# One doubling level fewer, running sums in halves, and a gate column block moved in a two-layer hybrid mixer

## The reference, cut to what matters

```python
p = rms_norm(x, norm_g) @ w_in                  # columns: sb, mla, rwkv, merge gates
# A) stick-breaking attention: between = reverse cumulative sum of log_fail over the keys
w = where(causal, exp(log_beta + between), 0);  y_sb = w @ v
# B) latent attention, softmax over chunk-causal scores
# C) RWKV-7: state = state * w_t + (state @ a_t) b_t + v_t k_t;  o_t = state @ r_t
merged = g_sb * (y_sb @ w_br_sb) + g_mla * (y_mla @ w_br_mla) + g_rw * (y_rw @ w_br_rw)
x = x + merged @ w_out
```

## Time and profile before

| | us |
|---|---|
| median of three runs | 1707.79 (1707.07 to 1709.06) |
| the profiled execution | 1707.07 |
| its span in the trace | 1705.3 |
| PE busy | 1690.0 |
| DVE busy | 1123.4 |
| ACT busy | 839.6 |
| POOL busy | 494.2 |

### The profile page before, as it was taken

One profiled execution on the slowest core, in us unless ns is written; L12 is line 12 of the kernel. 1 busy time (PEld: TensorE's weight loads), 2 busy tenths in 40 slices (PEclk: granted clock), 3 DMA queues, 4 the chain that ended last, 5 costly groups with the idle time before them and its releaser, 6 DMA issues.

```text
span 1705.3 us, 22326 instructions
## 1 busy us (share of the span) xinstructions
PE 1690.0 (99%) x8522; PEld 1409.5 (83%) x8522; DVE 1123.4 (66%) x1531; ACT 839.6 (49%) x1197; POOL 494.2 (29%) x728
## 2 busy tenths in 40 slices
PE   8999999999999999999999999999999999999999
PEld 7878888888878888888888788888888888888887
DVE  4667565755977556786656775756569666578853
ACT  6544454434544454555454444534445454555532
POOL 1011212410352426362410112232205334244500
PEclk9999999999999999999999999999999999999999
DMA  8866656556656556795687555556465555668764
GB/s 249 266 181 182 181 160 185 163 166 177 177 175 183 163 180 219 229 310 195 204 264 226 175 182 170 178 161 186 148 180 174 177 164 172 195 209 276 272 195 157
DMA packets 176914, 332.82 MB, mean 195 GB/s; under 512 B 19516, under 2 KB 32746, under 8 KB 176808
## 3 DMA queue, kind: packets, MB, share of 16 engines
q1 hardware_dynamic: 165416, 297.07, 57.2%
q0 software_dynamic: 9584, 33.47, 5.9%
q10 hardware_dynamic: 1808, 0.86, 0.2%
HBM read 311.18 MB, written 16.78 MB: 192 GB/s over the span
## 4 chain that ended last, share of the span: by engine, by line
PE 93%; DVE 4%; ACT 1%; DMA 1%; issue 1%; SPq 0%; ACTq 0%; DVEq 0%
PE D L698 83%; PE B L698 9%; DVE w_lo L1394 1%; DMA ring<-in_w_in 1%; DVE arena L1394 1%; ACT arena L1018 0%; ACT w_hi L1018 0%; DVE xy L1394 0%; PE B L890 0%; PE B L771 0%; DVE arena L1599 0%; DVE gev L1440 0%; PE B L869 0%; ACT gev L1018 0%; ACT L1018 0%
## 5 line engine op out<-in xcount | busy, mean ns | idle before, releaser
L1394 DVE TENSOR_TENSOR w_lo<-ring,w_hi 128x1024 fp32r<-128x1024 f32 (+3 forms) x560 | 677.6, 1221 | 357.5 <-ACT w_hi L1018 349.9
L1018 ACT ACTIVATE w_hi<-ring 128x1024 fp32r<-128x1024 f32 (+3 forms) x560 | 574.7, 1038 | 445.5 <-PE D L698 342.1
L698 PE MATMUL D<-w_hi,ht_hi 128*128 128x512 f32 (+2 forms) x1728 | 683.9, 396 | 4.1 <-DVE w_lo L1394 4.1
L698 PE MATMUL D<-w_hi,ht_lo 128*128 128x512 f32 (+2 forms) x1728 | 667.4, 386 | 0.0
L698 PE MATMUL D<-w_lo,ht_hi 128*128 128x512 f32 (+2 forms) x1728 | 666.6, 386 | 0.0
L698 PEld LDWEIGHTS D<-w_hi,ht_hi 128*128 128x128 f32 x1728 | 326.3, 189 | 71.8 <-issue 9.6
L698 PEld LDWEIGHTS D<-w_hi,ht_lo 128*128 128x128 f32 x1728 | 325.6, 188 | 65.7
L698 PEld LDWEIGHTS D<-w_lo,ht_hi 128*128 128x128 f32 x1728 | 326.4, 189 | 58.7 <-issue 0.5
L600 POOL COPY arena<-arena 32x256 f32<-32x256 f32 x240 | 168.7, 703 | 141.6 <-DVE arena L1424 105.9
L698 PEld LDWEIGHTS B<-arena 128*66 128x66 f32 (+3 forms) x1440 | 144.1, 163 | 25.5 <-issue 6.9
L1018 ACT ACTIVATE arena<-B 64x128 f32<-64x128 f32 (+5 forms) x162 | 54.5, 342 | 220.5 <-PE B L698 215.1
(11 more groups left out here) (156 smaller groups left out, 1380.5 us busy)
## 6 DMA issues: line engine op xcount, KB each, us to landing
ring<-in_w_in SPq DMA_DIRECT2D x368, 512.0 KB, 4.4
ring<-in_w_out SPq DMA_DIRECT2D x64, 512.0 KB, 5.4
ring<-in_w_br_mla SPq DMA_DIRECT2D x32, 512.0 KB, 5.1
gate_spill<-gev POOLq DMA_DIRECT2D x24, 512.0 KB, 4.7
arena<-gate_spill POOLq DMA_DIRECT2D x24, 512.0 KB, 5.8
ring<-in_mla_w_ukv SPq DMA_DIRECT2D x16, 512.0 KB, 4.2
ring<-in_w_br_rw SPq DMA_DIRECT2D x16, 512.0 KB, 5.2
ring<-in_w_br_sb SPq DMA_DIRECT2D x16, 512.0 KB, 5.0
```

The costliest lines, as they stand in the source:

```text
L698: return nc.tensor.matmul(o, a, b, start=start, stop=stop, skip_group_check=True)
L1018: return nc.scalar.activation(o, i, fn, **kw)
L1394: return v.tensor_tensor(o, a, b, op)
```

## The change

- The levels start from the inverse of 4x4 blocks instead of 2x2: `LEVELS` is 5, and DVE makes that inverse (products with three shifted diagonals, a reduction, transposes, six short operations, then a product of 512 columns and two sums). PE's first level visit stands 5 chunks behind the scores.
- The operands of both running sums are written as two fp32r halves (by DVE), the constants `inc`, `ntri`, `none` become an fp32r tile that POOL fills; twice as many matmuls in one pass each. The factor of the decay moves into ACT's scales.
- mg0 stands between sv and gate10: mg0 now ends at 184, gate10 at 192, gate11 at 200.
- The stick-breaking visits stand at 190, 194, 196.5 and 199, 202.5, 205.5. POOL does move(0) after mla pair 1; after move_heads(0) it goes to the end of gate10 (waits for its take-out and issues its spill), does all of move(1), and then enters the first pair with move_heads(1). `turn_heads` writes to a tile of its own.
- At the start SP's queue carries x and the first weights in turn (x0, w0, x1, w1, x2, w2, x3), and ACT and DVE split the first chunk ahead of the first columns.

```diff
-LEVELS = 6
-LEVELS_IN = 5
+LEVELS = 5
+LEVELS_IN = 4
...
-    g += wide("sq", C_SB) + pair(2) + wide("sk", C_SB + 512) + pair(3) + wide("sv", C_SB + 1024) + gates[10:]
-    g += wide("mg0", C_MG) + wide("mg1", C_MG + 512) + wide("sg", C_SB + 1536)
+    g += wide("sq", C_SB) + pair(2) + wide("sk", C_SB + 512) + pair(3) + wide("sv", C_SB + 1024) + wide("mg0", C_MG)
+    g += gates[10:] + wide("mg1", C_MG + 512) + wide("sg", C_SB + 1536)
...
-RW_STEPS = [1, 1.3, 1.2] + [0.9, 1] * LEVELS + [1] * 6
+RW_STEPS = [1, 1.2, 1, 1.5, 1.8] + [0.88, 0.98] * LEVELS + [0.85] * 6
...
-ML_STEPS += ML_PREP + ML_VISITS + [0.8] * 6 + ML_VISITS
-SB_STEPS = [4, 3.5, 3]
+ML_STEPS += ML_PREP + ML_VISITS + [1.05] * 6 + ML_VISITS
+SB_STEPS = [2.9, 1.2, 2.9, 2.7]
...
 sync:
             for j in range(4):
                 first_x(j)
+                if j < LEAD:
+                    first_chunk(j)
...
 gpsimd, layer 0:
+                    pool.dma_start(SUMS_IN, consts[:, K_END:K_END + 3 * P]).then_inc(sums_loaded, 16)
...
+                    nc.gpsimd.tensor_copy(sums_of[:], SUMS_IN.rearrange("p (n c) -> p n c", n=3)).then_inc(sums_in, 1)
...
 gpsimd, attention:
-                    if p == 0:
+                    if p == 1:
                         move(0)
                     beat(9)
...
                 move_heads(0)
-                dense_to(END["sv"])
+                dense_to(END["gate10"])
+                move(1)
                 for q in range(SBH // 2):
 
                     if q == 0:
                         move_heads(1)
-                    else:
-                        move(1, range(2))
-                    beat(2)
+                    beat(3)
                     for e in range(2):
                         pool.wait_ge(sb_act, 8 * l + 4 * q + 3 + e)
...
                     beat()
-                    if q == 1:
-                        pool.wait_ge(sb_pool, 4 * l + 4)
-                        move(1, range(2, 4))
...
 tensor, rw_pair:
-                beat()
-                beat()
+                beat(4)
                 for n in range(1, LEVELS + 1):
...
 tensor, sb_pair:
-                beat()
+                beat(2)
                 for e in range(2):
-                    lf, o = LF[e], B[2 * e + 1]
+                    o = B[2 * e + 1]
                     pe.wait_ge(sb_dve, 8 * l + 4 * q + e + 1)
-                    mm(o[:, 0:256], ntri, lf[:, 0:256], False, True)
-                    mm(o[:, 128:256], none, lf[:, 256:384], False, True)
-                    mm(o[:, 256:384], ntri, lf[:, 256:384], False, True).then_inc(sb_pe, 1)
+                    for lf in (LFH[e], LFL[e]):
+                        mm(o[:, 0:256], ntri, lf[:, 0:256], False, False)
+                        mm(o[:, 128:256], none, lf[:, 256:384], False, False)
+                        last = mm(o[:, 256:384], ntri, lf[:, 256:384], False, True)
+                    last.then_inc(sb_pe, 1)
...
 tensor, decay sums:
+                pe.wait_ge(sums_in, 1)
+                pe.wait_ge(sig_split, 2 * l + 2)
                 for h in range(HALVES):
-                    mm(B[h][:], con[:, K_INC:K_INC + P], SIG[:, h, :], True, True)
+                    mm(B[h][:], inc, SIGH[:, h, :], True, False)
+                    mm(B[h][:], inc, SIGL[:, h, :], False, True)
...
 scalar, start:
-            for n in range(LEAD):
-                for d0, m, src in pieces(0, n, 0):
-                    act.dma_start(ring[:, n, :, d0:d0 + m], src).then_inc(first_w[n], 16)
...
-                    columns_hi(0, first_pe, first_xh)
                     first_split(0)
+                    columns_hi(0, first_pe, first_xh)
...
 vector, rw_pair:
-                link(tt(WC, UC, first_c.unsqueeze(1).to_broadcast([P, 4, 32]), ALU.mult))
+                link(tt(WIDE[:, 0:3], UC.unsqueeze(1).to_broadcast([P, 3, 4, 32]), over_units(3), ALU.mult))
+                link(v.tensor_reduce(DIAG[:, :, 0:4], WIDE[:, 0:3], axis=X, op=ALU.add))
+                link(v.transpose(DIAG_T, DIAG))
+                d1, d2, d3 = (DIAG_T[:, k, :] for k in range(3))
+                t1, t2 = WIDE[:, 3, 0, :], WIDE[:, 3, 1, :]
+                tt(t1[:, 0:31], d1[:, 0:31], d1[:, 1:32], ALU.mult)
+                link(tt(t2[:, 0:30], d2[:, 0:30], d1[:, 2:32], ALU.mult))
+                tt(d2[:, 0:31], d2[:, 0:31], t1[:, 0:31], ALU.add)
+                link(tt(d3[:, 0:30], d3[:, 0:30], t2[:, 0:30], ALU.add))
+                link(tt(t1[:, 0:31], d1[:, 0:31], d2[:, 1:32], ALU.mult))
+                link(tt(d3[:, 0:31], d3[:, 0:31], t1[:, 0:31], ALU.add))
+                link(v.transpose(INVERSE[:, 0:3, :], DIAG_T))
+                beat()
+                link(tt(WIDE, over_columns(INVERSE, 4), over_units(4), ALU.mult))
+                link(tt(WIDE[:, 0:2], WIDE[:, 0:2], WIDE[:, 2:4], ALU.add))
+                link(tt(WC, WIDE[:, 0], WIDE[:, 1], ALU.add))
...
 vector, sb_pair, in the loop over e:
-                    last.then_inc(sb_dve, 1)
-                beat(2)
+                    link(last)
+                    link(v.tensor_copy(LFH[e], LF[e]))
+                    tt(LFL[e], LF[e], LFH[e].bitcast(F32), ALU.subtract).then_inc(sb_dve, 1)
+                    beat()
+                beat()
```

More of the change, by code:

```diff
@@ L63 @@
 LEAD = HALF_RING - 1
-ARENA = 19900
+ARENA = 20690
 SB_SCALE = 128.0 ** -0.5
@@ L76 @@
 K_END = K_COL + 2
+K_INC, K_NTRI, K_NONE = K_END, K_END + P, K_END + 2 * P
 def constants():
-    c = np.zeros((P, K_END), np.float32)
+    c = np.zeros((P, K_END + 3 * P), np.float32)
     i = np.arange(P)
@@ L85, in constants @@
     past_mid = (row <= MID).astype(np.float32)
-    c[:, K_INC:K_INC + P] = -DECAY * ((row <= col).astype(np.float32) - past_mid)
+    c[:, K_INC:K_INC + P] = (row <= col).astype(np.float32) - past_mid
     c[:, K_NTRI:K_NTRI + P] = -(row >= col).astype(np.float32)
@@ L90, in constants @@
     c[:, K_RWM:K_RWM + 512] = np.concatenate([strict, incl, strict, incl], 1)
[L91 to L98, removed]
+    for q in range(4):
+        r = slice(32 * q, 32 * q + 32)
+        for k in range(4):
+            at = K_LEV + 32 * k
+            c[r, at:at + 32] = ((col == row + (k + 1) % 4) & (row // 4 == col // 4))[r, r]
+        for n in range(LEVELS_IN):
+            b = 2 ** (n + 1)
+            joined = (row // (2 * b) == col // (2 * b)) & (row // b < col // b) | (n == 0)
+            at = K_LEV + 128 + 64 * n + 32 * (q % 2)
             c[r, at:at + 32] = joined[r, r]
-            if n == 0:
-                c[r, K_LEV:K_LEV + 32] = joined[r, r]
     half = ROPE // 2
@@ L176 @@
     assert ML_OUT[p - 2] < END[f"uq{p}"] <= END[f"ukv{p}"] <= ML_AT[p - 1] + 1
-assert END["sv"] <= ML_AT[4] < END["mg0"]
+assert END["sv"] <= ML_AT[4]
+assert ML_OUT[1] < END["mg0"]
 def merged_at(j):
@@ L293, in program @@
         AZ, LF = ([t[i] for t in sb_tiles] for i in (1, 2))
-        QK_OF = [xy[:, :, 0:512], QKT_T[:, 0:8, :].rearrange("p (a b) c -> p a (b c)", a=2)]
+        QK_OF = [xy[:, :, 0:512], again(at_tb, lambda: take(1280), lambda: take(1024))[1].rearrange("p (a c) -> p a c", a=2)]
+        HEADS_TURNED = QKT_T[:, 0:8, :].rearrange("p n c -> p (n c)")
         at_mkv = used[0]
@@ L324, in program @@
         ident = con[:, K_ID:K_ID + P]
-        first_c = con[:, K_LEV:K_LEV + 32]
-        level = [con[:, K_LEV + 32 + 64 * n:K_LEV + 96 + 64 * n] for n in range(LEVELS_IN)]
-        ntri, none = con[:, K_NTRI:K_NTRI + P], con[:, K_NONE:K_NONE + P]
+        diagonals = con[:, K_LEV:K_LEV + 128].rearrange("p (k c) -> p k c", k=4)
+        level = [con[:, K_LEV + 128 + 64 * n:K_LEV + 192 + 64 * n] for n in range(LEVELS_IN)]
+        SUMS_IN = AM.rearrange("p u c -> p (u c)")[:, 1664:2048]
+        inc, ntri, none = (sums_of[:, i, :] for i in range(3))
+        SIGH, SIGL = (t[:].rearrange("p (h k) t -> p h (k t)", h=HALVES) for t in (cqh, cql))
+        spare = mtl[:].rearrange("p k t -> p (k t)")[:, 2048:3584]
+        LFH, LFL = ([spare[:, i * 384:i * 384 + 384] for i in (2 * n, 2 * n + 1)] for n in range(2))
         cosx = con[:, K_COS:K_COS + 64].rearrange("p (h c) -> p h c", h=2)
@@ L430, in first_x, with first_chunk @@
                 sp.dma_start(xy[:, :, c], x[0, :, c].rearrange("(h p) d -> p h d", p=P)).then_inc(x_moved[j], 16)
+            def first_chunk(n):
+                for d0, m, src in pieces(0, n, 0):
+                    sp.dma_start(ring[:, n, :, d0:d0 + m], src).then_inc(first_w[n], 16)
             for j in range(4):
                 first_x(j)
+                if j < LEAD:
+                    first_chunk(j)
             for l in range(DEPTH):
@@ L590, in _, with move @@
                     beat(6)
-                def move(q, parts=range(4)):
-                    if parts[0] == 0:
-                        pool.wait_ge(blocks_turned[l], q + 1)
+                def move(q):
+                    pool.wait_ge(blocks_turned, 9 * l + q + 1)
                     turned = TURN[q >= 3].rearrange("p (h k j t) -> p h k j t", h=2, k=4, j=4)
```

(13 more changed lines are left out.)

81 lines of the change are left out of this document (45 added, 36 removed).

## The result

The changed kernel takes **1710.86 us** (median of 11 runs, 1709.69 to 1712.06) against 1707.07 for the kernel before on the same chip (11 runs): ratio 1.0022, 95% interval 1.0012 to 1.0031, so 3.8 us slower. The forecast was a change of +8.4 us, to 1716 from the 1707.79 that was known then. The profiled execution has a span of 1709.1 us, before 1705.3.

The account below looks back on a forecast made before the run. PE, busy 99% of the span, was taken as the bound. The terms -9.3 - 1.6 - 1.2 - 2.5 + 1.0 + 17.2 + 4.8 gave +8.4 us on 1707.79, so 1716 us, range 1697 to 1723.

Parts of the forecast that it names:

- Nothing else: Remaining effects, such as mg0's work and move(0) after the second pair: no cost or gain; uncovered, 1 to 2 us a layer.
- Longer DVE chain: DVE's 4x4 block inverse before the first level visit fits by half a microsecond: +1.0 us for eight pairs, 0 to +8.
- rival 4: DVE's chain before the first level is late too, 1 us for each of eight pairs: 1724 us; 9%.
- The stall: PE waits at its third stick-breaking visit for POOL's masks behind both moves, 8.6 us a layer: +17.2 us.
- The clock: PE's clock falls while it stands; 2.4 us lost after each stall, the start's price: +4.8 us.
- Rival 1: PE's clock doesn't fall in the stall: +3.6 us, 1711.4 us; 14%.
- The start: x and first weights alternate on one queue, weight split ahead of columns, first dense matmul before 10 us: -2.5 us.
- Decay sums: Four single-pass half matmuls replace four float32 passes on PE, 0.8 us saved twice: -1.6 us.
- Stick-breaking sums: Twelve half passes at 1.4 us replace 1.67 us, 128-column ones 0.11 apart, four visits: -1.2 us.
- Level: One doubling level fewer in the inverse saves 16 PE visits of 0.58 us each: -9.3 us.
- sums or level not shrinking: Halves costing as much as float32, or the level not shrinking, would be 3 us more, within the range.
- Rivals 2 and 3: Rival 2: short stall, clock stays, 1702.6 us, 6%. Rival 3: POOL isn't late, savings stand alone, 1694.2 us, 13%.

Follow-up runs that it names:

- experiments two and three: Two: changed kernel with move(0) back behind latent attention pair 0, 1714.87 us. Three: kernel before with move(0) behind pair 1, nothing else, 1703.96 us.
- Experiment eight: Changed kernel with move(1) not waiting for gate10's end, plus PE's first level visit 4.5 chunks behind the scores instead of 5: 1699.41 us.
- experiment nine: Changed kernel with move(1) not waiting for gate10's end, plus PE taking both running sums in float32 again: 1693.57 us, against 1689.24 without the latter.
- experiment four: Kernel before with the new start alone (x and first weights in turn on SP's queue, first weight split ahead of the columns): 1704.53 us.

## Why the prediction was wrong, and where it was right

The mechanism was right: the savings are real, one wait for POOL per layer takes them back, and the clock adds to it. The size was too high by 4.6 us, +8.4 against +3.8 (the range of 1697 to 1723 holds the 1710.9; a further 0.7 us is the old kernel's median, 1707.79 then and 1707.07 over 11 runs). Most of the 4.6 is one step.

- **"Nothing else: ... move(0) after the second pair leaves POOL free earlier."** This is the step that failed. Its place was looked at only from POOL's side, as a change of when POOL is free, and costed at nothing. It was worth 3.0 to 4.0 us (experiments two and three), because the copies no longer met DVE's preparation of the second latent attention pair, which stands ahead of the first pair's softmax, and PE waited for that softmax. The earlier trace rows showed that wait, 2.2 us for ACT at L890, and the step did not ask what made ACT late.
- **Longer DVE chain, +1.0:** nothing in the trace, and the level alone came to -10.8 rather than -9.3 + 1.0. The reasoning on the slack was right (0.45 us measured); at such a slack the likeliest cost was zero, not a microsecond. Experiment eight shows how near rival 4 was.
- **The stall, 17.2:** 16.5. Of its parts, `move(1)` took 11.42 beside the splits (11.0 forecast), `move_heads(1)` 7.18 with DVE silent (8.3 forecast); it began at 602.36, 9.3 after PE's first visit (593.03), as forecast. The collision assumed for the second move did not happen. The first 16 copies are 0.71 each, the second 16 0.45, both on the same engine in the same 19 us: this trace bears out the Trainium skill (SBUF — State Buffer, section Who interferes with whom), which has a VectorE instruction with two SBUF inputs contend with a GpSimd instruction that reads SBUF.
- **The clock, 4.8:** 4.1 (twice 2.07). Taking the start's price was right to within 0.4 us a stall, with some luck, as other rests gave between 1.7 and 2.9. Rival 1 fell: its number, 1711.4, is next to the measured one only because what the forecast left out made up for the clock.
- **The start, -2.5:** -2.7 alone. The first dense matmul was forecast before 10 us and came at 10.21, because the second half of the transposes waited for x. **Decay sums, -1.6:** -1.6 in the visits. **Stick-breaking sums, -1.2:** -1.4; the 128-column matmuls in fp32r lie at the 0.06 end of their bounds behind another such, not at 0.11, and at 0.17 behind a 256-column one. **Level, -9.3:** -10.8 with an interval that holds 9.3. The forecast's remark that sums or level not shrinking would cost 3 us covers the sums only (2.8); the level would have been 9.3, outside the range.
- **Rivals 2 and 3** (short stall, POOL not late) fell with the 8.3 us.

Put together from the traces and runs, with `move(0)` at 1.65 a layer from the timelines: -9.3 - 1.6 - 1.4 - 2.7 - 3.3 + 16.5 + 4.1 = +2.3, against +3.8. The 1.5 us left over are about the small losses of dense work read in the trace (positions 35 to 45, 0.5 a layer, and 0.8 at the layer boundary); what causes those was not tried. With the level at its measured -10.8 the gap is 3.0; the 1.5 between the two readings of the level lie within that run's interval.

The three changes of the old kernel measured alone make -10.8 - 3.0 - 2.7 = -16.5. The halves add -3.1 by their visits, -4.3 as measured in experiment nine, so -19.6 or -20.8; the kernel with all of them and no stall has -18.5. They add up, to within the intervals.

## What to carry to other kernels

When a large block of work is moved, write the helper engine's program out in its new order, with the wait that heads it: here one line that waits for a dense position stood ahead of 32 copies, and moving it turned +3.8 us into -18.5. When a step moves, ask also whom it no longer disturbs in its old place, and start from a wait in the old profile. And where PE stood for 2.2 us or longer here, it lost some 2 us more behind that (1.7 to 2.9), whether it had stood for 2.2 or for 8.3, so a stall of 2.7 us cost 4.5. PE's waits of 1.6 us and less in experiment eight cost nothing beyond themselves.

## What the runs showed of the hardware

- TensorE's granted clock fell with a rest of 8.3, 4.5 and also 2.7 us, and with one of 2.2 us at the start of experiment four's trace (granted clock 0.51 from 35.7 to 39.2). With the rest of 2.7, PE first went on at the upper level for 1.4 us and the clock fell during the work (from 617.0 on), so the drop is not tied to the moment of restart. The slow stretch lasted 4.0 us after the longest rest, 5.3 after that of 4.5 (617.29 to 622.58) and 3.5 after the two shortest. Behind the six waits of 0.8 to 1.6 us in experiment eight's level visits the matmuls kept the spacing of the upper level (dense ones 0.23 apart). That is the direction of the Trainium skill (TensorE: Matmul & The Clock Gate, section What's actually happening), by which idleness throttles the array and sustained activity releases it; that the array slows down after it has already resumed was new to me.
- POOL's copy of 32x256 took 0.45 us with DVE silent and 0.71 beside the splits; and DVE's 128-column operations with two operands in SBUF took 0.29 alone, 0.37 beside POOL's copies. The loss runs both ways. DVE's transposes of one operand took 1.29 us for two, with the copies or without.
